# Weight columns interleaved in pairs, one buffer for the low halves of h, one order of products

## The reference, cut to what matters

```python
def modulate(x, g, c_act, w, b):
    m = c_act @ w + b
    shift, scale, gate = jnp.split(m, 3, axis=-1)
    h = rmsnorm(x, g) * (1.0 + scale[:, None, :]) + shift[:, None, :]
    return h, gate[:, None, :]

def swiglu(h, w_gate, w_up, w_down):
    return (jax.nn.silu(h @ w_gate) * (h @ w_up)) @ w_down
...
        h, g = modulate(x, norm_g[i, 0], c_act, mod_w[i, 0], mod_b[i, 0])
        x = x + 0.5 * g * swiglu(h, ffn_w_gate[i, 0], ffn_w_up[i, 0], ffn_w_down[i, 0])
```

## Time and profile before

| | us |
|---|---|
| median of 3 runs | 1782.38 (1781.78 to 1782.6) |
| span of the profiled execution | 1789.0 |
| TensorE busy, products (98% of the span) | 1749.9 |
| TensorE busy, weight loads (95%) | 1700.5 |
| VectorE busy (81%) | 1452.8 |
| ScalarE busy (53%) | 956.5 |

### The profile page before, as it was taken

One profiled execution on the slowest core, in us unless ns is written; L12 is line 12 of the kernel. 1 busy time (PEld: TensorE's weight loads), 2 busy tenths in 40 slices (PEclk: granted clock), 3 DMA queues, 4 the chain that ended last, 5 costly groups with the idle time before them and its releaser, 6 DMA issues.

```text
span 1789.0 us, 34260 instructions
## 1 busy us (share of the span) xinstructions
PE 1749.9 (98%) x14686; PEld 1700.5 (95%) x14686; DVE 1452.8 (81%) x1749; ACT 956.5 (53%) x1254; POOL 0.2 (0%) x4
## 2 busy tenths in 40 slices
PE   5999999999999999999999999999999999999999
PEld 4999999998999999999999999999999998989999
DVE  7799898888898889898557989765899887567766
ACT  4443466665533354445766444565655556775553
POOL 0000000000000000000000000000000000000000
PEclk9999999999999999999999999999999999999999
DMA  9998834344597949895444989343288545415551
GB/s 396 414 419 307 322 141 154 134 173 154 219 410 312 373 167 386 326 393 193 170 152 186 388 329 378 134 163 139 110 304 292 206 147 177 151 73 214 187 197 37
DMA packets 68149, 426.23 MB, mean 238 GB/s; under 512 B 7488, under 2 KB 10832, under 8 KB 31824
## 3 DMA queue, kind: packets, MB, share of 16 engines
q1 hardware_dynamic: 63936, 416.22, 60.5%
q10 hardware_dynamic: 4112, 8.62, 1.4%
HBM read 423.74 MB, written 3.17 MB: 239 GB/s over the span
## 4 chain that ended last, share of the span: by engine, by line
PE 90%; DVE 4%; ACT 3%; DMA 2%; issue 0%; DVEq 0%; SPq 0%; ACTq 0%
PE bank L1573 24%; PE bank L1574 24%; PE bank L1575 24%; PE bank L1630 2%; PE bank L1632 2%; PE bank L1631 2%; DMA raw<-weights 1%; PE bank L1686 1%; PE bank L1989 1%; DMA mix<-mods 1%; PE bank L1586 1%; PE bank L1600 1%; PE bank L1589 1%; PE bank L1822 1%; ACT w_hi L495 1%; DVE work L1034 1%
## 5 line engine op out<-in xcount | busy, mean ns | idle before, releaser
L1573 PE MATMUL bank<-h_hi,w_hi 128*128 128x256 f32 x2504 | 696.0, 278 | 0.0
L1574 PE MATMUL bank<-h_lo_rest,w_hi 128*128 128x256 f32 x2504 | 694.9, 278 | 0.0
L1575 PE MATMUL bank<-h_hi,w_lo 128*128 128x256 f32 x2504 | 694.8, 277 | 0.0
L913 DVE TENSOR_TENSOR w_lo<-raw,w_hi 128x2048 fp32r<-128x2048 f32 x267 | 609.5, 2284 | 90.4 <-ACT w_hi L495 89.3
L495 ACT ACTIVATE w_hi<-raw 128x2048 fp32r<-128x2048 f32 x276 | 527.9, 1913 | 160.0 <-PE bank L1575 145.7
L1573 PEld LDWEIGHTS bank<-h_hi,w_hi 128*128 128x128 f32 x2504 | 472.8, 189 | 0.0
L1574 PEld LDWEIGHTS bank<-h_lo_rest,w_hi 128*128 128x128 f32 x2504 | 470.2, 188 | 0.0
L1575 PEld LDWEIGHTS bank<-h_hi,w_lo 128*128 128x128 f32 x2504 | 470.1, 188 | 0.0
L1573 PE MATMUL bank<-a_hi,w_hi 128*128 128x256 f32 x1280 | 358.5, 280 | 1.2 <-DVE a_lo L1291 0.8
L1575 PE MATMUL bank<-a_hi,w_lo 128*128 128x256 f32 x1280 | 355.3, 278 | 0.0
L1574 PE MATMUL bank<-a_lo,w_hi 128*128 128x256 f32 x1280 | 355.3, 278 | 0.0
(11 more groups left out here) (303 smaller groups left out, 1989.4 us busy)
## 6 DMA issues: line engine op xcount, KB each, us to landing
raw<-weights SPq DMA_DIRECT2D x276, 1024.0 KB, 5.4
modws<-mods SPq DMA_DIRECT2D x144, 768.0 KB, 6.6
mix<-mods SPq DMA_DIRECT2D x5, 1024.0 KB, 8.8
mix<-mods ACTq DMA_DIRECT2D x8, 512.0 KB, 13.3
biases<-scratch ACTq DMA_DIRECT2D x1, 2048.0 KB, 13.1
mix<-biases ACTq DMA_DIRECT2D x4, 512.0 KB, 4.0
modws<-mods SPq DMA_DIRECT2D x1, 1024.0 KB, 11.7
x<-xin SPq DMA_DIRECT2D x1, 1024.0 KB, 10.9
```

The costliest lines, as they stand in the source:

```text
L913: eng.tensor_tensor(w_lo[g % NW][:, :], raw[g % NRAW][:, :], w_hi[g % NW][:, :], ALU.subtract).then_inc(sems["wlo"], 1)
L1573: eng.matmul(dst, ah, bh, start=start, stop=False, skip_group_check=skip)
L1574: eng.matmul(dst, ah, bl, start=False, stop=False, skip_group_check=skip)
L1575: return eng.matmul(dst, al, bh, start=False, stop=stop, skip_group_check=skip)
```

## The change

The host interleaves the columns. In a block of an input matrix the 256 columns of a chunk are stored in pairs, column c of the first 128 beside column c of the second 128, so that the 128 weights of a product are every other float of 256 (1024 bytes). In a block of an output matrix each group of 256 columns is stored in this way. The V blocks, whose w is the moving operand, keep their order through `moving`. The products are the same ones, with a step of two floats in their weights; the filling products too. The low half of h becomes one buffer, `h_lo_all`, with the space of both gaps behind it, and the products of kk = 0 in `gemm` have the order of all others. The remaining places in the diff (`first`, the first up block, `early_out`, `last`) only write `part` in the new way.

```diff
--- before
+++ after
@@ -264,14 +264,12 @@
         h_hi = sb("h_hi", [P, KT, T], F32R)
-        h_lo_rest = sb("h_lo_rest", [P, KT - 1, T], F32R)
-        gap = sb("gap", [P, 16])
-        h_lo_first = sb("h_lo_first", [P, T], F32R)
-        gap2 = sb("gap2", [P, 48])
+        h_lo_all = sb("h_lo_all", [P, KT, T], F32R)
+        gap2 = sb("gap2", [P, 64])

         def h_lo(kk):

-            return h_lo_rest[:, kk - 1, :] if kk else h_lo_first[:, :]
+            return h_lo_all[:, kk, :]
...
-        z_hi, z_lo = h_hi[:, 1:3, :], h_lo_rest[:, 0:2, :]
+        z_hi, z_lo = h_hi[:, 1:3, :], h_lo_all[:, 1:3, :]
@@ -1576,41 +1574,42 @@
             def gemm(dst, st, i=0, a=0, b=0, tokens=False, first=False, between=None):

-                hi, lo = [w.rearrange("p (k n) -> p k n", k=KT) for w in begin(st, i, a, b)]
-                both = [(m, slice(m * P, (m + 1) * P), dst[:, m * T:(m + 1) * T]) for m in range(2)]
+                hi, lo = [w.rearrange("p (k n) -> p k n", k=KT) if tokens else
+                          w.rearrange("p (k c m) -> p k m c", k=KT, m=2) for w in begin(st, i, a, b)]
+                both = [(m, slice(m * P, (m + 1) * P) if tokens else m, dst[:, m * T:(m + 1) * T]) for m in range(2)]
...
@@ -1619,30 +1618,21 @@
-                            if tokens and kk == 0:
-                                eng.matmul(d, h_lo(kk)[:, part], hi[:, kk, :], start=True, stop=False)
-                                eng.matmul(d, h_hi[:, kk, part], hi[:, kk, :], start=False, stop=False)
-                                eng.matmul(d, h_hi[:, kk, part], lo[:, kk, :], start=False, stop=False)
-                            elif tokens:
+                            if tokens:
                                 mm = three(d, h_hi[:, kk, part], h_lo(kk)[:, part], hi[:, kk, :], lo[:, kk, :],
                                            kk == 0, kk == KT - 1)
-                            elif kk == 0:
-                                eng.matmul(d, hi[:, kk, part], h_lo(kk), start=True, stop=False)
-                                eng.matmul(d, hi[:, kk, part], h_hi[:, kk, :], start=False, stop=False)
-                                eng.matmul(d, lo[:, kk, part], h_hi[:, kk, :], start=False, stop=False)
                             else:
-                                mm = three(d, hi[:, kk, part], lo[:, kk, part], h_hi[:, kk, :], h_lo(kk),
+                                mm = three(d, hi[:, kk, part, :], lo[:, kk, part, :], h_hi[:, kk, :], h_lo(kk),
                                            kk == 0, kk == KT - 1)
                 mm.then_inc(sems["blk"], 1)

             def gemm_out(st, i=0, a=0, b=0, ready=None, fresh=False):

-                hi, lo = [w.rearrange("p (k n) -> p k n", k=2) for w in begin(st, i, a, b)]
+                hi, lo = [w.rearrange("p (k j c m) -> p k j m c", k=2, j=4, m=2) for w in begin(st, i, a, b)]
                 for kk in range(2):
                     ready(kk)
                     for m in range(KT):
-                        part = slice(m * P, (m + 1) * P)
-                        mm = three(acc(m), hi[:, kk, part], lo[:, kk, part], a_hi[:, kk, :], a_lo[:, kk, :],
+                        mm = three(acc(m), hi[:, kk, m // 2, m % 2, :], lo[:, kk, m // 2, m % 2, :], a_hi[:, kk, :], a_lo[:, kk, :],
                                    fresh and kk == m % 2 == 0, False, True)
...
@@ -1690,9 +1680,11 @@
-                hi = begin(st, 0, 0, 0)[0].rearrange("p (k n) -> p k n", k=KT)
+                hi = begin(st, 0, 0, 0)[0]
+                turned_hi = hi.rearrange("p (k c m) -> p k m c", k=KT, m=2)
                 for n in range(FILL.get(st, 14)):
-                    eng.matmul(bank[5][:, 0:T], hi[:, n % KT, 0:P], hi[:, n % KT, :], start=True, stop=True)
+                    at = n % KT * T
+                    eng.matmul(bank[5][:, 0:T], turned_hi[:, n % KT, 0, :], hi[:, at:at + T], start=True, stop=True)
...
@@ -2133,11 +2124,15 @@
     def wide(w):
         n = w.shape[1] // 256
+        return w.reshape(KT, P, n, 2, P).transpose(2, 1, 0, 4, 3).reshape(n, P, 2048)
+
+    def moving(w):
+        n = w.shape[1] // 256
         return w.reshape(KT, P, n, 256).transpose(2, 1, 0, 3).reshape(n, P, 2048)

     def deep(w):
         n = w.shape[0] // 256
-        return w.reshape(n, 2, P, D).transpose(0, 2, 1, 3).reshape(n, P, 2048)
+        return w.reshape(n, 2, P, 4, 2, P).transpose(0, 2, 1, 3, 5, 4).reshape(n, P, 2048)
@@ -2156,7 +2151,7 @@
     def attn(w, wo):
-        pipelined([wide(w[:, :D]), wide(w[:, D:2 * D]), wide(w[:, 2 * D:])], deep(wo))
+        pipelined([wide(w[:, :D]), wide(w[:, D:2 * D]), moving(w[:, 2 * D:])], deep(wo))
```

More of the change, by code:

```diff
@@ L1585, in gemm @@
                         for m, part, d in both:
-                            eng.matmul(d, hi[:, kk, part], h_hi[:, kk, :], start=kk == m == 0, stop=False,
+                            eng.matmul(d, hi[:, kk, part, :], h_hi[:, kk, :], start=kk == m == 0, stop=False,
                                        skip_group_check=True)
                             if st:
-                                eng.matmul(d, lo[:, kk, part], h_hi[:, kk, :], start=False, stop=False,
+                                eng.matmul(d, lo[:, kk, part, :], h_hi[:, kk, :], start=False, stop=False,
                                            skip_group_check=True)
@@ L1599, in gemm @@
                         for m, part, d in both:
-                            mm = eng.matmul(d, hi[:, kk, part], h_lo(kk), start=False, stop=kk == KT - 1,
+                            mm = eng.matmul(d, hi[:, kk, part, :], h_lo(kk), start=False, stop=kk == KT - 1,
                                             skip_group_check=True)
@@ L1605, in gemm @@
                         for m, part, d in both:
-                            eng.matmul(d, hi[:, kk, part], h_lo(kk), start=kk == m == 0, stop=False,
+                            eng.matmul(d, hi[:, kk, part, :], h_lo(kk), start=kk == m == 0, stop=False,
                                        skip_group_check=True)
-                            eng.matmul(d, hi[:, kk, part], h_hi[:, kk, :], start=False, stop=False,
+                            eng.matmul(d, hi[:, kk, part, :], h_hi[:, kk, :], start=False, stop=False,
                                        skip_group_check=True)
@@ L1612, in gemm @@
                         for m, part, d in both:
-                            mm = eng.matmul(d, lo[:, kk, part], h_hi[:, kk, :], start=False, stop=kk == KT - 1,
+                            mm = eng.matmul(d, lo[:, kk, part, :], h_hi[:, kk, :], start=False, stop=kk == KT - 1,
                                             skip_group_check=True)
@@ L1739, in early_out @@
             def early_out(st, m0, m1):
-                hi, lo = [w.rearrange("p (k n) -> p k n", k=2) for w in begin(st, 0, 0, NBLK[stages[st]] - 1)]
+                hi, lo = [w.rearrange("p (k j c m) -> p k j m c", k=2, j=4, m=2) for w in begin(st, 0, 0, NBLK[stages[st]] - 1)]
                 k.wait("alo", st, b=2 * GROUPS[stages[st]] - 2)
                 for m in range(m0, m1):
-                    part = slice(m * P, (m + 1) * P)
-                    three(acc(m), hi[:, 0, part], lo[:, 0, part], a_hi[:, 0, :], a_lo[:, 0, :], False, False, True)
+                    three(acc(m), hi[:, 0, m // 2, m % 2, :], lo[:, 0, m // 2, m % 2, :], a_hi[:, 0, :], a_lo[:, 0, :], False, False, True)
             def last(st, ready, early=0, token_squares=None):
-                hi, lo = [w.rearrange("p (k n) -> p k n", k=2) for w in begin(st, 0, 0, NBLK[stages[st]] - 1)]
+                hi, lo = [w.rearrange("p (k j c m) -> p k j m c", k=2, j=4, m=2) for w in begin(st, 0, 0, NBLK[stages[st]] - 1)]
                 ffn = stages[st] in ("ffn", "cffn")
@@ L1762, in last @@
                     for n in range(14):
-                        eng.matmul(bank[5][:, 0:T], hi[:, 0, 0:P], hi[:, 0, 0:T], start=True, stop=True)
+                        eng.matmul(bank[5][:, 0:T], hi[:, 0, 0, 0, :], w_hi[(k.block(st) + NBLK[stages[st]] - 1) % NW][:, 0:T],
+                                   start=True, stop=True)
                 ready()
@@ L1768, in last @@
                         squares(st + 1, 0)
-                    part = slice(m * P, (m + 1) * P)
                     for kk in range(1 if m < early else 0, 2):
-                        mm = three(acc(m), hi[:, kk, part], lo[:, kk, part], ahi[:, kk, :], alo[:, kk, :],
+                        mm = three(acc(m), hi[:, kk, m // 2, m % 2, :], lo[:, kk, m // 2, m % 2, :], ahi[:, kk, :], alo[:, kk, :],
                                    False, False, True)
```

## The result

The changed kernel takes 1849.5 us (median of 4 runs, 1848.5 to 1851.5) against 1782.4 (1781.8 to 1782.6): a ratio of 1.0363, 95% interval 1.0342 to 1.0384. It is 67 us slower, where 23 us faster was forecast, and the time lies 31.5 us above the range.

The account below looks back on a forecast made before the run. TensorE was taken as bound by product count times distance, 113.3 or 117.8 ns. Heads 6.6, long state 15.3 and other blocks 1.9 us made 24, less 1: span 1766, median 1759 us, range 1706 to 1814 with a little for spread.

Parts of the forecast that it names:

- (c): Interleaved weights and moving operand advance at equal pace in one fixed relation; every product at 113.3 ns, between 110 and 119.
- (e): VectorE and DMA loads nearing their limit between 73 and 209 us once products are 113.3 ns apart; 1 us taken off.
- R1: Rival, faster, chance 0.18: equal pace frees both read streams of each other; 110 ns a product, 1717 us, or 1706 at 109.
- R2: Rival, slower, chance 0.29: one bad stream relation for every product, 117.6 to 119 ns, 1814 to 1832 us; loses above 115.2 ns.
- (a): Three separately ordered products beginning each half of an input block; one buffer and order save 0.055 us a block, 6.6 us.
- (b): 72 blocks in the long state (117.8 ns between products) brought to the short one (113.3 ns): 15.3 us, other blocks 1.9.
- (d): Counts of products, weight loads, DMAs and waits, and the ScalarE and VectorE instructions, stay the same, at no price.
- R3: Rival: the two levels come from something else, only the heads go, 1776 us; chance 0.10 as faster, 0.07 as no change.
- R4: Rival, slower, chance 0.04: loading every other value halves the load rate, over 220 ns a product, 3160 us.

Follow-up runs that it names:

- The experiment at 80 bytes: The changed kernel with h_hi, h_lo, a_hi and a_lo moved to start 80 instead of 192 bytes beyond the weights, modulo 256: 1822.9 us, ratio 1.0212 to the kernel before.
- The probes: Small kernels without the computation, issuing products of the kernel's shape with varied weight step and relative position of moving operand: 113.3 to 122.3 ns a product with neighbouring weights.
- the version at 112 bytes: The kernel before with one h_lo buffer, one order of products, no interleaving, and moving operands 112 bytes beyond the weights, modulo 256: 1772.8 us, ratio 0.9941.
- The last probe: Computation-free kernel: loads almost alone at steps 1, 2, 3, 4 and 8, then neighbouring weights with 128 moving values each read twice: 111.7 ns for the latter.
- the first probe: Computation-free kernel: blocks of 48 products, neighbouring or every other weight, at varied byte offsets: 113.3 to 120.0 ns for neighbours, 117.8 to 121.1 for every other.

## Why the prediction was wrong

**(c), the interleaving: this step failed.** The term that it put at nothing is the load with a step. It took 113.3 ns for a product whose load has a step, on the ground that the shape keeps this distance today. The load of that shape is another one. Its own interval is 117.8 ns, and with products beside it at the kernel's positions 120.0. In the forecast's own sum, 12,900 products x (120.0 - 113.3) = 86 us replace the nothing that stood there, and less the 24 us assumed as saved that makes +62 us, 1844 us beside the 1849.5 measured (VectorE has time again at that pace, so the 1 us of (e) goes). Rows 12 had a warning that was read as a bound for the good end only: L1653, with one moving value, is loads alone, and its 112 ns say that at 113.3 TensorE already has the loads at its heels. With a cover of 1 to 2 ns, an edit that touches the load can't be costed at nothing. The upper bound of 119 ns, from contention rows, had no row of a strided load in it; it was 1 ns short of what came.

**The reasoning about equal pace held in one half.** (c) expected one fixed relation and one level, and one level came: 120.0 ns in every stage. That equal pace also frees the streams of each other, R1's mechanism, isn't shown. With interleaved weights both streams cover 1024 bytes in a product, and the distance still went from 117.8 to 121.1 ns by position. The 111.7 ns at all 16 positions came where each moving value was read twice, which halves the reads as well. What neither (c) nor R1 asked is what the load costs by itself in the new layout.

**R2, the fixed collision, had the direction and half of the mechanism.** "A weight load that covers twice as many bytes may ask for more of the memory" stood there as its reason, and 119 ns, 1832 us, as its upper price. The experiment at 80 bytes splits it: 33 us by the load, at any position tried, and 28 us by the collision. Its break-even of 115.2 ns was sound: the best that any position left to the interleaving, 117.8, is above it.

**The position rule was off by a factor of two.** The prediction took relations modulo 128 bytes. The probes have period 256: 0 and 128 differ (120.0 and 118.6), so do 112 and 240 (113.3 and some 117.1), and 0, 256, 512 and 768 agree. The shifts by 144 bytes to 80 and by 176 to 112 say where h and a lie without them: at 192 bytes from w (80 - 144 and 112 - 176, modulo 256) in the kernel before and in the changed one, which is one of the three positions with a 113.3 level and, in the probe, also a 117.8 one. That agrees with the two levels of rows 4 and 5.

**(a), the heads,** were read right as rows (the two heads of a block cost 0.055 us in the short state) and wrong as a saving. Without them the median rose by 16 us instead of falling by 6.6. I take it that a head restarts the relation of the streams twice in a block and so ends a long stretch; that is argued and not tested. The condition that the step named, "if the state doesn't get worse by it", is what happened.

**(b) and the sum** counted the long state twice. The profiled run of the kernel before had a span of 1789.0 us. Its later runs give time and span together: a run of 1782.71 us has a span of 1780.9. The run's own time is thus the span plus 1.8 us, and the profiled execution would have been a run of 1790.8. That is 8 us above the median. I take it that more of its blocks were long, 8 / 0.21 = 38 of the 72; no execution at the median was traced, so this isn't shown. The forecast took off all 72 and then moved to the median by subtracting 6.6 again. The same steps without that give 1789.0 - 23 + 1.8 = 1768, and the version at 112 bytes reached 1773. The part was real, 10 us in the median instead of 23.

**(d)** holds: the counts are the same, 14,686 products and loads. **(e)**, VectorE and the DMAs slipping at a shorter distance, couldn't be seen in the changed kernel, which is slower. In the version at 112 bytes, from 45 to 200 us, the products run at 113 ns with VectorE at 139.18 of 155 us, the DMA share at 0.98 and TensorE without a gap, so in that stretch the cover held.

**R3** (nothing locks) is out: the distance became one value everywhere, and the probes move it by position alone. **R4** is out for step 2, but not for step 4, whose 233.3 ns are twice 111.7 and more.

**The rules of the Trainium skill.** The probes have loads of neighbours at 111.7 ns and of every other value at 117.8. By the Trainium skill (SBUF — State Buffer, section "Door 1: The DMA port swizzle", the note on cachelines) two hits in a 16-byte line keep the full rate. The runs speak against that at step 2 by 6.1 ns, and for its lines beyond it. Loads with steps 2, 3, 4 and 8 touch 64, 96, 128 and 128 stretches of 16 bytes, and 117.8, 173.3, 233.3 and 237.8 ns are 1.81 to 1.86 ns for each. The last probe's expectation asked this of steps 3 and 8, and both came out so, 8 within 4.5 ns of 4. By this count (an estimate from four intervals) 64 stretches already take longer than the 111.7 ns of neighbours, so step 2 costs 6 ns and not twice the time. By the Trainium skill (TensorE: Matmul & The Clock Gate, section "LDWEIGHTS (loading the stationary operand)") the time goes by the count of columns alone; for the same 128 columns the runs have 111.7 to 237.8 ns. By the Trainium skill (SBUF — State Buffer, section "Who interferes with whom") TensorE's two read ports are independent; the runs have 113.3 to 120.0 ns by position alone, at one clock, so the two streams of reads aren't.

## What to carry to other kernels

Where TensorE streams short products, compare the distance of two products with that of two weight loads alone before an edit touches the layout of weights: here 113.3 against 111.7 ns, so of a load that takes 6 ns more every product pays all but those 1.6 ns. Keep weights as neighbours and tune the position of the moving operand instead; it needs no change of layout and here brought 10 us in the median, of the 23 that the interleaving was to bring. And before a stall seen in one profiled execution is subtracted from a median, ask whether the median run has it at all: compare span with span.

## What the runs showed of the hardware that I had not expected

- The interval of loads of 128 fp32r weights, alone and at the upper clock, by step: 111.7 ns (1), 117.8 (2), 173.3 (3), 233.3 (4), 237.8 (8). Beside 512 moving columns steps 1 and 2 are alike, 233.3 ns for step 2 and 229 to 233 for step 1, so there the price of step 2 is hidden.
- A load with step 4 takes 233.3 ns at either level of the clock (granted 1.00 and 0.50), where one of neighbours goes from 111.7 to 213.3.
- Products of 256 moving fp32r columns, each with a load of neighbours, have a distance that depends on the relative position of both operands modulo 256 bytes: 120.0 at 0, 113.3 at 112, and at 64 and 192 two levels, 113.3 and 117.8, of which a block takes one and keeps it. What is special about these three I can't say.
- When each moving value is read twice, this dependence is gone: 111.7 ns at all 16 positions, with neighbouring weights.
- A run of products with two moving columns, with the loads back to back, ended with the clock at 1.2 GHz (0.50 in the first probe's window at 394 us). There steps 1 and 2 cost the same, 213.3 ns.
